# Three cache copies issued by ScalarE on its own DMA queue, and the merge gates loaded by SyncE

## The reference, cut to what matters

```
h = rmsnorm(x)
qA kA vA | qB kB vB | gate_a gate_b = h @ w_in
branch A: stick-breaking attention, paged cache for the samples
branch B: dilated window attention, three groups (window, dilation) = (128,1), (512,4), (2048,16)
x = x + (sigmoid(gate_a) * (oA @ w_br_a) + sigmoid(gate_b) * (oB @ w_br_b)) @ w_o
x = x + hier_moe(rmsnorm(x))          32 experts, 2 per token
y = rmsnorm(x)
new_kv_b{g}_sample = concat(cache_kv_b{g}[:, 1:], new row)   for each of the 8 samples
```

## Time and profile before

| | us |
|---|---|
| median of 3 runs | 1618.66 |
| lowest and highest | 1617.77, 1618.89 |
| the profiled execution | 1622.56 |
| its span, first to last instruction | 1620.7 |
| PE busy | 1204.8 (74%) |
| DVE busy | 587.9 (36%) |
| POOL busy | 280.2 (17%) |
| ACT busy | 242.6 (15%) |
| DMA, mean rate | 281 GB/s |

### The profile page before, as it was taken

How to read it: one execution, slowest core, us unless ns; L and a number is a source line. 1 busy time by engine, 2 the same in 40 slices (tenths; PEclk the granted TensorE clock), 3 DMA queues, 4 the chain that set the end, 5 groups by cost and what they waited for, 6 DMA issues and landing times. The chain is left out here.

```text
span 1620.7 us, 14617 instructions
## 1 busy us (share of the span) xinstructions
PE 1204.8 (74%) x5502; PEld 699.6 (43%) x5502; DVE 587.9 (36%) x763; ACT 242.6 (15%) x393; POOL 280.2 (17%) x208
## 2 busy tenths in 40 slices
PE   4999999895699899843005997459878788777780
PEld 4878888784245444421004644423233233323230
DVE  2299999963543444350001213511011111111114
ACT  2121111002343343100000010011110101111112
POOL 1055555530033223000000000001101010101110
PEclk9999999998699989856557997579999999999995
DMA  6389989993567767665546405249999999999974
GB/s 197 131 297 340 328 304 335 362 351 118 232 253 287 277 234 275 225 251 202 213 207 231 166 0 211 118 161 410 408 410 404 407 410 401 411 403 407 404 282 175
DMA packets 99542, 455.44 MB, mean 281 GB/s; under 512 B 12768, under 2 KB 44816, under 8 KB 56832
## 3 DMA queue, kind: packets, MB, share of 16 engines
q1 hardware_dynamic: 73176, 300.09, 47.5%
q0 software_dynamic: 25776, 150.45, 24.9%
q10 hardware_dynamic: 544, 4.26, 0.7%
HBM read 442.10 MB, written 65.44 MB: 313 GB/s over the span
## 5 line engine op out<-in xcount | busy, mean ns | idle before, releaser
L423 PE MATMUL proj_ps<-hT,w_slots 128*128 128x260 f32 x1472 | 332.8, 387 | 8.5 <-ACT stage L446 6.1
L423 PEld LDWEIGHTS proj_ps<-hT,w_slots 128*128 128x128 f32 x1472 | 280.2, 192 | 58.9 <-issue 15.0
L1661 PE MATMUL ex_gp<-raw,ex_xT 128*64 128x512 f32 x1024 | 232.0, 601 | 21.3 <-DMA raw<-in_w_up_e 13.2
L1675 PE MATMUL ex_yp<-raw,ex_hmT 128*64 128x512 f32 x512 | 139.2, 693 | 69.0 <-DMA raw<-in_w_down_e 68.5
L209 POOL DMA_INDIRECT ring<-in_cache_k_a,run_sb x64 | 138.9, 2171 | 192.5 <-DVE scores L481 164.3
L474 DVE TENSOR_TENSOR ring<-ring,q_rep 128x2048 f32<-128x2048 f32 x64 | 145.9, 2281 | 41.1 <-ACT q_rep L465 41.1
L481 DVE TENSOR_REDUCE scores<-ring 128x32 f32<-128x2048 f32 x64 | 145.8, 2280 | 0.0
L1661 PEld LDWEIGHTS ex_gp<-raw,ex_xT 128*64 128x64 f32 x1024 | 70.6, 138 | 158.8 <-issue 123.7
L1180 PE MATMUL mg_ps<-oT,mg_wb 128*128 128x260 f32 x192 | 45.0, 399 | 125.2 <-DMA mg_wb<-in_w_br_b 125.2
L1616 DVE TENSOR_TENSOR ex_hm<-ex_sg,ex_gp 64x512 f32<-64x512 f32 x32 | 21.7, 680 | 267.5 <-ACT ex_sg L1596 267.5
L209 POOL DMA_INDIRECT ring<-in_cache_v_a,run_sb x64 | 73.4, 1146 | 255.7 <-PE at_vp L695 240.4
(11 more groups left out here) (239 smaller groups left out, 1063.3 us busy)
## 6 DMA issues: line engine op xcount, KB each, us to landing
raw<-in_w_gate_e SPq DMA_DIRECT2D x64, 1024.0 KB, 21.6
raw<-in_w_up_e SPq DMA_DIRECT2D x64, 1024.0 KB, 27.5
raw<-in_w_down_e SPq DMA_DIRECT2D x64, 1024.0 KB, 26.0
o_kvs<-in_cache_kv_b SPq DMA_DIRECT2D x1, 32752.0 KB
w_slots<-in_w_in SPq DMA_DIRECT2D x23, 1024.0 KB, 8.5
o_kvs<-in_cache_kv_b SPq DMA_DIRECT2D x1, 8176.0 KB
kv<-in_cache_kv_b SPq DMA_DIRECT2D x24, 256.0 KB, 6.0
gate_rows<-stage SPq DMA_DIRECT2D x16, 260.0 KB, 8.7
```

Of the source, the lines that this page charges most:

```text
L423: last = pe.matmul(pp[:, j, half, 0:H], w[:, m % 2, c, j * P:(j + 1) * P], k.hT[:, c, half * H:(half + 1) * H], start=(c == 0), stop=(c == ...
L1661: last = pe.matmul(gp[at:at + SLOT, j], xT[:, c, :], raw[:, slot, c1 * FF:(c1 + 1) * FF], start=(c == 0), stop=(c == KC - 1))
L1675: last = pe.matmul(yp[h * SLOT:(h + 1) * SLOT, j], hmT[:, c, :], raw[:, slot, o:o + 512], start=(c == 0), stop=(c == FC - 1))
```

## The change

The three shifts are issued by ACT instead of SP: those of groups 0 and 1 ahead of ACT's work in `weigh_a`, that of group 2 as ACT's first instruction in `decode_b`. The gates of `merge` are loaded by SP instead of ACT, behind the weights of the first four tiles and ahead of the last four's; the second half still waits until the first has landed, but there is no longer a wait for the fourth tile's weights. SP's loop in `merge` is unrolled.

```diff
@@ weigh_a
             @block.sync
             def _(sp):
                 sp.dma_start(k.tables_b[:], k.io["consts"][:, k.at["rel"][0]:k.at["row_bias"][0]]).then_inc(tables_in, 16)
-                for g in range(NG - 1):
-                    shift(k, sp, g)
                 sp.wait_ge(tables_in, 16)
...
             @block.scalar
             def _(act):
+                for g in range(NG - 1):
+                    shift(k, act, g)
                 act.wait_ge(s["clamped"], 1)
@@ decode_b
                     for g, (_, d) in enumerate(GROUPS):
                         sp.dma_start(k.kv[:, b, g, :], k.io[f"cache_kv_b{g}"][0, b].rearrange(
                             "(n d) k h e -> n d (k h e)", d=d)[:, 0, :]).then_inc(kv_in, 16)
-                shift(k, sp, NG - 1)
...
             @block.scalar
             def _(act):
+                shift(k, act, NG - 1)
                 act.wait_ge(s["scores"], 2)
@@ merge
             @block.sync
             def _(sp):
-                with sp.Fori(0, TRIPS) as i:
+                for i in range(TRIPS):
                     for j in range(BUFS):
-
-                        sp.wait_ge(s["yb"], i * BUFS + (j + 1))
-                        at = i * (BUFS * P) + j * P
+                        t = i * BUFS + j
+                        sp.wait_ge(s["yb"], t + 1)
                         sp.dma_start(wb[:, j, 0:CA], k.io["w_br_a"][0].rearrange("(c p) n -> p c n", p=P)[
-                            :, :, bass.ds(at, P)]).then_inc(w_in[j], 16)
+                            :, :, t * P:(t + 1) * P]).then_inc(w_in[j], 16)
...
+                    if i == 0:
+                        for n in range(TRIPS):
+                            if n:
+                                sp.wait_ge(s["gates_in"], 16 * n)
+                            c = slice(n * BUFS, (n + 1) * BUFS)
+                            sp.dma_start(gate[:, :, c], k.io["gates"].rearrange("p (k c) n -> p k c n", k=2)[:, :, c])\
+                                .then_inc(s["gates_in"], 16)

             @block.scalar
             def _(act):
-
-                act.wait_ge(w_in[BUFS - 1], 32)
-                for i in range(TRIPS):
-                    if i:
-                        act.wait_ge(s["gates_in"], 16 * i)
-                    c = slice(i * BUFS, (i + 1) * BUFS)
-                    act.dma_start(gate[:, :, c], k.io["gates"].rearrange("p (k c) n -> p k c n", k=2)[:, :, c])\
-                        .then_inc(s["gates_in"], 16)
-
```

## The result

The changed kernel takes 1664.01 us in the median of 4 runs (1659.88 to 1667.67), the kernel before 1618.22 in the median of 4 (1611.17 to 1618.89): a ratio of 1.0292, 95% interval 1.0253 to 1.0331. It is slower, and 1665 was predicted. The profiled execution took 1665.81 us with a span of 1664.0; before it was 1622.56 and 1620.7, so profile against profile the change cost 43.3 us.

A forecast was written before the change was run, and what follows sets the result against it. The 32 MB shift ahead of merging's weights on SP's queue was taken to bound the kernel, PE waiting 125 us. Terms +48, -2 and 0 gave +46: 1669 profiled, 1665 on the runs' scale, likeliest case's range 1650 to 1682.

The forecast's parts named there:

- both waits: DVE's 17.76 us for the `kv` loads in decode and PE's 125.18 us for `mg_wb` in merging, behind the 32 MB shift.
- Part 1: 32 MB shift moved to ACT's queue: `kv` delayed beside it, decode's products 167.5 us late, merging's PE start net +48 us.
- the bounds: Packet time 10 us down or 8 up, hanging issues 2 more, start, landing and clock 5 either way; range 1650 to 1682.
- 912 with its terms: Merging's first issue at 912, second load's issue 0.51 later, weights landing 3.8 after that: PE starts at about 916.8.
- The 1 us of completion: Allowance in decode between the last `kv` packets and their landing, put at about 868.
- The rule one for one: An engine serves two queues packet for packet whatever their size, so each small `kv` packet waits for one of 65.5 KB; 0.84.
- the first rival: An engine serves a load's 9 packets together per turn: `kv` at 766, PE at about 819, -25 us, 1594; chance 0.07.
- Equal bytes: Rival: two queues halve an engine's rate, so merging's PE starts at about 767, -94 us, 1525; chance 0.07.
- ACT's queue is one of its own: ACT's loads show as q10, apart from SP's; were it not so, `kv` would land at 870, the same +48.
- Part 2: Merging's gates loaded by SP: at DVE about 8 us after PE's start, second four tiles' weights hidden; -2 us with the clock.
- The clock: PE, coming from decode's products after some 6 us break, may keep the upper level in merging instead of 0.50.
- Part 3: Two small shifts issued by ACT before its table load, sharing engines with `tables_b`: cost 0 to 2 us, taken as 0.

## Why the prediction was right

**What bounded the kernel** was read rightly: without the shift both waits are gone, and with them 117 us.

**Part 1** held in its mechanism and was 6 us too large. Predicted was PE's start in merging 48 us later; it came 910.79 - 868.74 = 42.1 later. The steps: decode as a whole began 1.8 us earlier, which no part of the sum had (half of it was there before `weigh_a`, where nothing was changed: `tables_b` is issued at 388.41, before at 389.34); from there DVE's first product was 165.5 us later than before and not 167.5; from it to merging's first issue it took 43.3 and not 44.0; and from that to PE's start 3.4 and not 4.8. Each is within the bounds given. Two sums were off by little: 912 with its terms, 0.51 and 3.8, is 916.3 and not 916.8, and the bounds add up to 1650 to 1680, not 1682. The 1 us of completion stood in no row; here the last `kv` packet ended 0.6 us before DVE's product. The wait of DVE was put at "some 185" and is 183.2. SP's issues hung, as feared, but the loads that were left to issue cost nothing visible beyond that.

**The rule one for one**, taken over from a stretch with 8.3 KB and 0.5 KB packets, is shown for 65.5 KB beside 2 KB in two kernels (127 to 127, 181 to 182), beside the 0.5 KB of merging's weights (97 to 97) and for 8 KB (225 per engine). With it the first rival falls, whole transfers per turn: `kv` landed at 864, not 766. Counts over a long stretch would be equal too if both queues took turns of nine packets, a case that the prediction did not tell from the first rival; the single turn, eight to eight on eight engines, rules it out. The section "Queues, rings and completion order" of the Trainium skill's page "DMA: Bandwidth & Descriptors", which says that a turn typically holds some 9 to 17 descriptors, is not what these two queues did, so far as the profile's packets are descriptors. Equal bytes falls too: 8.32 MB against 0.23. That ACT's queue is one of its own is seen in q10's 127 packets beside q1's.

**Part 2** was put at -2 and is nothing that can be told. The gates moved alone gave 0.9997; in the changed kernel the tiles took 957.98 - 910.79 = 47.2 us up to the output projection, against 46.8 before. Two steps of it failed. The clock did not keep the upper level over the break: PE was busy 1.21 us of the 4 from 908, and in the next 6 the granted clock was 0.58, little better than the 0.50 of the earlier trace rows. And the gates reached DVE 11.1 us after PE's start, not 8: PE itself started 1.4 us sooner after merging's first issue than put, and the first half came 10.3 us after its issue and not 9.1, with the DMA engines 0.99 busy at 314 GB/s. That the weights of the four tiles slowed it fits this but was not tested. The second four tiles' weights did arrive in time: PE ran all 192 matmuls of the tiles in one group of 45.39 us.

**Part 3** at 0 was right; moved alone the small shifts gave 0.9991, and the stage has its 24.4 us.

**The sum.** +46 was forecast, and profile against profile +43.3 came: 42.1 until PE's start, 0.4 in the tiles, 0.9 behind them (the stages behind the projection are 42 to 43 later: `rt_g_row` is issued at 1029.62, before at 987.21). That the medians lie 45.8 apart, and the forecast 1 us from the median, is luck: the profiled executions lie 4.3 and 1.8 us above their medians, and that fills what the terms fell short by. What the prediction didn't see is how little held the shift where it was: it weighed only the change, while 118 us lay in the idle DMA engines of the output projection and behind it.

## What to carry to other kernels

In these runs a queue of its own (ACT's beside SP's) gave a transfer a turn per packet and not a share of the bytes: small loads beside it on the same engines paid one large packet for each of theirs. Before moving a bulk copy, count the packets per engine that will be queued beside it, multiply by the time of a large one, and ask which work used to run beside the copy and no longer will. Better is a stretch in which the DMA engines are idle and compute is not, with the copy cut to fit it and its outermost dimension cut so that all engines share it.

## What the runs showed that was not expected

- An issue can hang while its queue drains slowly: SP 176.91 us in the 24 `kv` loads, ACT about 123 us in the second transfer of the shift of 1 KB packets. On ACT the engine's own work stands behind it.
- From memory to memory, eight engines moved 208 GB/s and sixteen 333: a 65.5 KB packet took 2.5 us in the one case and 3.1 in the other.
- Pieces of 8,188 bytes took 0.74 us each beside `kv`, 11 GB/s an engine, and 0.49 later, where the 65.5 KB ones moved 26; the cause is open.
